# Experts of a mixture layer in steps of 1024, 1024, 1024 and 512 feed-forward columns instead of seven steps of 512

## The chip, the cores and the metric

One core of one Trainium2 chip runs the whole program. The metric is the device time of one execution in microseconds (us). A matmul on TensorE (PE) has a weight load (PEld) and a multiplication; DVE is VectorE, ACT is ScalarE, SP is SyncE, whose queue issues the weight transfers. All data is float32, and the trace shows every float32 matmul of the code as two weight loads and two matmuls.

## The reference, cut to what matters

The program computes two transformer blocks over 256 tokens of width 1024. The part that the change touches is the mixture of experts at the end of the first block: eight experts, two chosen for each token, each a gated feed-forward layer with 3584 hidden columns.

```python
def expert_block(args):
    tok, e = args
    xb = xf[tok]
    hb = jax.nn.silu(xb @ w_gate[e]) * (xb @ w_up[e])     # 1024 -> 3584
    return hb @ w_down[e]                                 # 3584 -> 1024
...
out = jnp.zeros((T, D), jnp.float32).at[row_tok].add(y)   # y: rows times the gate of the token
```

## The kernel before

**Weights.** All large weights of the program go through one ring in SBUF, `weight_ring`, of 6 slots (SLOTS) with 2048 floats on each of 128 partitions (SLOTW), so 1 MB a slot. SP fills them in a fixed order (`load`, line 304). Before it issues the load with number q it waits until `slots_used` says that PE has finished with load q - 6. PE waits for a slot's own semaphore (`landed`), does the slot's matmuls, and adds one to `slots_used`. So SP runs at most six slots ahead, and the order of the loads is the order in which PE uses them.

**One expert.** The tokens of an expert, at most 96 (CAP), lie feature-major in `hcur` (8 chunks of 128 features by 96 tokens). DVE copies them there and signals `tokens_ready`. The 3584 hidden columns are done in STEPS_M = 7 steps of 512. A step s has six slots: two of gate weights (each 4 of the 8 feature chunks by 512 columns, so rows of 512 floats in HBM), two of up weights, and two of down weights (256 rows of 1024 floats each). An expert has 42 slots.

**Engines in a step.** `gate_up_wide` (matmuls on line 723) sums gate and up into PSUM banks 2(s%2) and 2(s%2)+1, so two sets of banks take turns. ACT takes tanh of the gate bank (`step`, line 1166, into THS). DVE multiplies (1 + tanh) by gate (line 1464, into AAS, `gate_ready`) and that by up (line 1461, into HBS, `hidden_ready`). `down_wide` (matmuls on line 738) of step s-1 comes after gate and up of step s and adds into banks 4 and 5. The factor one half of silu is applied elsewhere.

**Order on PE for an expert.** Gate and up of step 0; `turn` (8 transposes of the expert before, line 749); gate and up of step 1; `scatter(0)` (line 760, adds half of the tokens of the expert before); down 0; `scatter(1)`; then a hardware loop `pe.Fori` of two passes, each with steps 2+2i and 3+2i and the downs behind them; then gate and up of step 6, down 5 and down 6. All this is the body of an outer hardware loop over the 8 experts. SP, ACT and DVE have loops of the same form.

Of the kernel before, what the change touches and what calls it, by code (L numbers as in the profile page):

```python
# [15 lines left out]
P = 128  # L16
# [7 lines left out]
SLOTS = 6  # L24
# [7 lines left out]
MCOLS = 512  # L32
STEPS_M = 3584 // MCOLS
MOE_SLOTS = 6 * STEPS_M

# [54 lines left out]
def fused_two_blocks(nc, ins, out):  # L90
# [4 lines left out]
    with ExitStack() as ctx:  # L95
# [66 lines left out]
        HBS = SC[:, 1, :, :].rearrange("p a b -> p (a b)")[:, 0:8 * CAP].rearrange("p (a f c) -> p a f c", a=2, f=4)  # L162
# [133 lines left out]
        def _(sp):  # L296
# [22 lines left out]
            def experts(wg, wu, wd):  # L319

                q0 = SLOT["moe"]

                def columns_of(w, e, s, j):
                    return w[bass.ds(e * KT + 4 * j, 4), :, bass.ds(s * MCOLS, MCOLS)].rearrange("k p n -> p k n")

                def rows_of(e, s, j):
                    return wd[bass.ds((e * (2 * STEPS_M) + s * 2 + j) * COLS, COLS), :].rearrange("(f p) n -> p f n", p=P)

                with sp.Fori(0, NEXP) as e:
                    ec = e * MOE_SLOTS  # L330
                    for j in range(2):
                        load(q0 + j, columns_of(wg, e, 0, j), 4, ec)
                    for j in range(2):
                        load(q0 + 2 + j, columns_of(wu, e, 0, j), 4, ec)
                    with sp.Fori(0, STEPS_M - 1) as i:
                        x = ec + i * 6
                        for j in range(2):
                            load(q0 + 4 + j, columns_of(wg, e, i + 1, j), 4, x)
                        for j in range(2):
                            load(q0 + 6 + j, columns_of(wu, e, i + 1, j), 4, x)  # L340
                        for j in range(2):
                            load(q0 + 8 + j, rows_of(e, i, j), 2, x)
                    for j in range(2):
                        load(q0 + MOE_SLOTS - 2 + j, rows_of(e, STEPS_M - 1, j), 2, ec)
# [203 lines left out]
        def _(pe):  # L548
# [155 lines left out]
            def moe():  # L704
# [7 lines left out]
                def gate_up_wide(q, s, rounds, wait):  # L712

                    for b in range(2):
                        bank = ps[:, 2 * (s % 2) + b, :]
                        for j in range(2):
                            w = landed(q + 2 * b + j, rounds).rearrange("p (k n) -> p k n", k=4)
                            if b == 0 and j == 0:
                                pe.wait_ge(sem("hidden_ready"), wait)
                            for m in range(4):  # L720
                                for k in range(4):
                                    for c in (0, 64):
                                        mm = pe.matmul(bank[c:c + 64, m * CAP:(m + 1) * CAP],  # L723
                                                       w[:, k, m * P + c:m * P + c + 64], hcur[:, 4 * j + k, :],
                                                       start=(j == 0 and m == 0 and k == 0), stop=(j == 1 and k == 3),
                                                       skip_group_check=True)
                            mm.then_inc(sem("slots_used"), 1)

                def down_wide(q, s, rounds, ready, start, stop):

                    for j in range(2):
                        w = landed(q + j, rounds).rearrange("p (f n) -> p f n", f=2)
                        if j == 0:
                            pe.wait_ge(sem("hidden_ready"), ready)
                        for f in range(2):
                            for d in range(KT):
                                for c in (0, 64):
                                    mm = pe.matmul(ps[c:c + 64, 4 + d // 4, (d % 4) * CAP:(d % 4 + 1) * CAP],  # L738
                                                   w[:, f, d * P + c:d * P + c + 64], HBS[:, s % 2, 2 * j + f, :],
                                                   start=(start and j == 0 and f == 0 and d % 4 == 0),  # L740
                                                   stop=(stop and j == 1 and f == 1), skip_group_check=True)
# [22 lines left out]
                with pe.Fori(0, NEXP) as e:  # L764
                    es, ea = e * (MOE_SLOTS // SLOTS), e * STEPS_M
                    pe.wait_ge(sem("tokens_ready"), e + 1)
                    gate_up_wide(q0, 0, es, a0 + ea)
                    turn(e)
                    gate_up_wide(q0 + 4, 1, es, a0 + ea)
                    scatter(0, e)  # L770
                    down_wide(q0 + 8, 0, es, a0 + 1 + ea, True, False)
                    scatter(1, e)
                    with pe.Fori(0, (STEPS_M - 2) // 2) as i:
                        for j in range(2):
                            s = 2 + j
                            x = ea + i * 2
                            gate_up_wide(q0 + 6 * s - 2, s, es + i * 2, a0 + s - 1 + x)
                            down_wide(q0 + 6 * s + 2, s - 1, es + i * 2, a0 + s + x, False, False)
                    s = STEPS_M - 1
                    gate_up_wide(q0 + 6 * s - 2, s, es, a0 + s - 1 + ea)  # L780
                    down_wide(q0 + 6 * s + 2, s - 1, es, a0 + s + ea, False, False)
                    down_wide(q0 + 6 * s + 4, s, es, a0 + s + 1 + ea, False, True)
# [339 lines left out]
        def _(act):  # L1122
# [38 lines left out]
            def step(s, q, ready, n=512, over="", buf=TH):  # L1161
# [4 lines left out]
                act.activation(buf[:, s % 2, :], ps[:, 2 * (s % 2), 0:n], ACT.Tanh, scale=0.5).then_inc(  # L1166
# [14 lines left out]
            def moe():  # L1181
                q0, a0 = SLOT["moe"], steps_done[0]
                n = 4 * CAP
# [5 lines left out]

                act.memzero(yfeat).then_inc(sem("expert_out_copied"), 1)  # L1190
                with act.Fori(0, NEXP) as e:
                    es, ea = e * MOE_SLOTS, e * STEPS_M
                    step(0, q0 + 1 + es, a0 + ea, n, buf=THS)
                    rows(e)
                    step(1, q0 + 5 + es, a0 + ea, n, buf=THS)
                    with act.Fori(0, (STEPS_M - 2) // 2) as i:
                        for j in range(2):
                            s = 2 + j
                            step(s, q0 + 6 * s - 1 + es + i * 12, a0 + s - 1 + ea + i * 2, n, buf=THS)
                    s = STEPS_M - 1  # L1200
                    step(s, q0 + 6 * s - 1 + es, a0 + s - 1 + ea, n, buf=THS)
# [231 lines left out]
        def _(dve):  # L1433
# [59 lines left out]
            def step(s, q, done, n=512, over="", th=TH, aa=AA, hb=None, up=1):  # L1493
# [3 lines left out]
                stt(aa[:, p, :], th[:, p, :], 1.0, ps[:, 2 * p, 0:n], ALU.add, ALU.mult).then_inc(  # L1497
                    sem("gate_ready" + over), 1)
                dve.wait_ge(sem("gate_ready" + over), done + 1)
                dve.wait_ge(sem("slots_used" + over), q + 1 + up)  # L1500
                h = (HB if hb is None else hb)[:, p, :, :].rearrange("p f t -> p (f t)")
                tt(h, aa[:, p, :], ps[:, 2 * p + 1, 0:n], ALU.mult).then_inc(sem("hidden_ready" + over), 1)
# [26 lines left out]
            def moe():  # L1529
                q0, a0 = SLOT["moe"], steps_done[0]  # L1530
                n = 4 * CAP
# [524 lines left out]
```

## Time and the profile before

| | before |
|---|---|
| median of 3 runs | 2909.37 us |
| lowest, highest | 2905.66, 2914.35 us |
| the profiled execution: its time | 2908.74 us |
| its span | 2907.0 us |
| experts, first to last gate/up/down matmul | 604.4 to 1602.5 us |

The span is that of the profiled execution; its own time is 1.74 us longer. Of the span the experts hold about 998 us. "Issue" is idle time of an engine for which the profile shows no releaser. The group "q8 instruction" of the DMA view is the traffic that brings program code, and "us to landing" is the median from the issue of a load to its last byte.

### The profile page before, as it was taken

The numbers are of one execution on the slowest core, as the hardware profiler recorded it, in microseconds if no ns is written. First come the engines' busy times: TensorE is split into PE (matmuls) and PEld (weight loads), VectorE is DVE, ScalarE is ACT, GpSimd is POOL, SyncE is SP. The second block draws the span as 40 slices with busy tenths as digits, with TensorE's granted clock in tenths as the row PEclk, the third lists the DMA queues.
The fourth block names the chain that finished last, engine by engine and source line by source line (L and its number), as shares of the span: only waits on it lengthen the run. The fifth ranks groups of instructions, "written<-read, shape, count | busy, mean of one in ns | idle before, by whom it ended". The sixth has DMA issues, their size and how long they took to land.

```text
span 2907.0 us, 64519 instructions
## 1 busy us (share of the span) xinstructions
PE 2653.3 (91%) x29724; PEld 2267.7 (78%) x29724; DVE 505.9 (17%) x949; ACT 284.9 (10%) x668; POOL 49.6 (2%) x117
## 2 busy tenths in 40 slices
PE   8799998799999999999999897789999997789998
PEld 7577767589989898898989776677776776677775
DVE  2210006420001000010100223222000224221001
ACT  1200003100000000000000122220000122210000
POOL 5000000000000000000000000000000000000000
PEclk9899999799999999999999898899999998899999
DMA  7234453259899999999989452123444452123442
GB/s 211 87 130 152 151 170 105 87 217 387 323 351 364 333 382 329 364 351 348 366 328 384 147 160 91 59 82 123 157 149 154 139 159 73 62 89 129 158 145 79
DMA packets 347811, 586.96 MB, mean 202 GB/s; under 512 B 13508, under 2 KB 187784, under 8 KB 347608
## 3 DMA queue, kind: packets, MB, share of 16 engines
q1 hardware_dynamic: 341400, 581.00, 57.0%
q8 instruction: 186, 3.05, 0.4%
q10 hardware_dynamic: 5728, 2.27, 0.3%
q0 software_dynamic: 480, 0.50, 0.2%
q14 instruction: 17, 0.14, 0.0%
HBM read 582.69 MB, written 1.05 MB: 201 GB/s over the span
## 4 chain that ended last, share of the span: by engine, by line
PE 89%; DVE 4%; ACT 4%; issue 3%; POOL 0%; DMA 0%; DVEq 0%; SPq 0%; ACTq 0%
PE ps L723 21%; PE ps L657 17%; PE ps L606 12%; PE ps L596 12%; PE ps L738 10%; PE ps L673 9%; PE ps L580 2%; PE ps L588 2%; PE ps L760 1%; ACT scores L1232 1%; PE ps L830 1%; PE ps L953 1%; DVE scores L1464 1%; DVE small L1601 1%; ACT heads_feat L1139 0%
## 5 line engine op out<-in xcount | busy, mean ns | idle before, releaser
L723 PE MATMUL ps<-heads_feat,weight_ring 128*64 128x96 f32 x14336 | 617.5, 249 | 37.6 <-issue 36.8
L723 PEld LDWEIGHTS ps<-heads_feat,weight_ring 128*64 128x64 f32 x14336 | 609.5, 140 | 46.7 <-issue 46.7
L657 PE MATMUL ps<-h_feat,weight_ring 128*128 128x256 f32 x2304 | 503.8, 380 | 0.0
L657 PEld LDWEIGHTS ps<-h_feat,weight_ring 128*128 128x128 f32 x2304 | 438.6, 191 | 72.5 <-issue 14.4
L606 PE MATMUL ps<-h_feat,weight_ring 128*128 128x256 f32 x1216 | 298.0, 409 | 46.2 <-ACT probs_feat L1139 45.3
L606 PEld LDWEIGHTS ps<-h_feat,weight_ring 128*128 128x128 f32 x1216 | 250.0, 208 | 88.7 <-issue 48.8
L738 PE MATMUL ps<-scores,weight_ring 128*64 128x96 f32 x7168 | 308.7, 246 | 11.1 <-issue 11.1
L738 PEld LDWEIGHTS ps<-scores,weight_ring 128*64 128x64 f32 x7168 | 300.3, 137 | 19.6 <-issue 19.6
L596 PE MATMUL ps<-weight_ring,h_feat 128*128 128x256 f32 x1312 | 292.0, 385 | 3.7 <-DVE h_feat L1461 3.1
L596 PEld LDWEIGHTS ps<-weight_ring,h_feat 128*128 128x128 f32 x1312 | 253.1, 194 | 40.1 <-DVE h_feat L1461 4.0
L673 PE MATMUL ps<-weight_ring,scores 128*128 128x512 f32 x576 | 252.6, 592 | 0.0
L1464 DVE SCALAR_TENSOR_TENSOR gelu_tmp<-gelu_tmp,ps 128x384 f32<-128x384 f32 (+1 forms) x92 | 55.8, 606 | 1067.7 <-ACT gelu_tmp L1166 1067.7
L673 PEld LDWEIGHTS ps<-weight_ring,scores 128*128 128x128 f32 x576 | 109.4, 190 | 123.7 <-issue 122.0
L1166 ACT ACTIVATE gelu_tmp<-ps 128x384 f32<-128x384 f32 (+1 forms) x92 | 48.9, 532 | 1450.3 <-PE ps L723 774.8
L1461 DVE TENSOR_TENSOR scores<-gelu_tmp,ps 128x384 f32<-128x384 f32 (+1 forms) x92 | 55.8, 606 | 429.8 <-PE ps L723 230.2
L580 PE MATMUL ps<-ident,stage 128*128 128x128 f32 x276 | 53.8, 362 | 49.1 <-ACT stage L1156 42.0
L580 PEld LDWEIGHTS ps<-ident,stage 128*128 128x128 f32 x276 | 41.5, 184 | 63.6 <-ACT stage L1156 33.0
L606 PE MATMUL ps<-heads_feat,weight_ring 128*128 128x256 f32 x384 | 83.4, 380 | 1.4 <-ACT heads_feat L1139 1.4
L606 PEld LDWEIGHTS ps<-heads_feat,weight_ring 128*128 128x128 f32 x384 | 72.8, 190 | 12.0 <-ACT heads_feat L1139 2.2
L596 PE MATMUL ps<-weight_ring,heads_feat 128*128 128x256 f32 x256 | 60.9, 400 | 8.3 <-DVE heads_feat L1461 7.6
L596 PEld LDWEIGHTS ps<-weight_ring,heads_feat 128*128 128x128 f32 x256 | 50.8, 201 | 18.3 <-DVE heads_feat L1461 5.6
L491 POOL TENSOR_TENSOR small<-small 128x2 f32<-128x2 f32 (+2 forms) x14 | 16.4, 1174 | 2757.9 <-DVE small L1475 1878.1
(265 smaller groups left out, 1066.9 us busy)
## 6 DMA issues: line engine op xcount, KB each, us to landing
weight_ring<-in_moe_w_gate SPq DMA_DIRECT2D x112, 1024.0 KB, 7.4
weight_ring<-in_moe_w_up SPq DMA_DIRECT2D x112, 1024.0 KB, 7.9
weight_ring<-in_moe_w_down SPq DMA_DIRECT2D x112, 1024.0 KB, 7.9
weight_ring<-in_w_ffn SPq DMA_DIRECT2D x66, 1024.0 KB, 5.2
weight_ring<-in_w_in SPq DMA_DIRECT2D x30, 1024.0 KB, 5.3
weight_ring<-in_w_merge SPq DMA_DIRECT2D x24, 1024.0 KB, 5.1
weight_ring<-in_ffn_w_gate SPq DMA_DIRECT2D x14, 1024.0 KB, 5.0
weight_ring<-in_ffn_w_up SPq DMA_DIRECT2D x14, 1024.0 KB, 5.0
```

The source lines that it names most:

```text
L580: mm = pe.transpose(bank[0:width, m * T + t * P:m * T + t * P + kin], src(m, t), ident[0:kin, 0:kin])
L588: mm = pe.matmul(out_[c:c + 64], lhs[:, c:c + 64], rhs, start=start, stop=stop)
L596: mm = (paired if n < P else pe.matmul)(bank[:, t * n:(t + 1) * n], lhs(k, t), w[:, k, :], start=(k == 0), stop=(k == kt - 1))
L606: mm = pe.matmul(bank[:, m * T:(m + 1) * T], w[:, k, m0 + m * P:m0 + (m + 1) * P], rhs(k), start=(k == 0), stop=(k == kt - 1))
L657: mm = pe.matmul(bank[:, m * n:(m + 1) * n], w[:, k, m * P:(m + 1) * P], rhs[:, k, :], start=(k == 0), stop=(k == KT - 1))
L673: mm = pe.matmul(ps[:, 4 + 2 * t + h, :], HB[:, s % 2, f, t * P:(t + 1) * P], w[:, f, h * 512:(h + 1) * 512], start=(start and f == 0), st ...
L723: mm = pe.matmul(bank[c:c + 64, m * CAP:(m + 1) * CAP], w[:, k, m * P + c:m * P + c + 64], hcur[:, 4 * j + k, :], start=(j == 0 and m == 0 ...
L738: mm = pe.matmul(ps[c:c + 64, 4 + d // 4, (d % 4) * CAP:(d % 4 + 1) * CAP], w[:, f, d * P + c:d * P + c + 64], HBS[:, s % 2, 2 * j + f, :] ...
L760: mm = pe.matmul(ps[:, 6 + h, :], gcur[0:CAP, t * P:(t + 1) * P], ycur[0:CAP, h * 512:(h + 1) * 512], start=True, stop=True)
L1166: act.activation(buf[:, s % 2, :], ps[:, 2 * (s % 2), 0:n], ACT.Tanh, scale=0.5).then_inc(sem("tanh_ready" + over), 1)
L1461: return dve.tensor_tensor(o, a, b, op)
L1464: return dve.scalar_tensor_tensor(out=o, in0=a, scalar=s, in1=b, op0=op0, op1=op1)
```

## The change

The same 42 slots are cut otherwise. A step of 1024 columns has four slots of gate (each 2 feature chunks by 1024 columns, so rows of 4 KB), four of up and four of down; the last step has 512 columns and is as before (two slots each, rows of 2 KB). Gate sums go to banks 0 and 1, up sums to banks 2 and 3, in every step, with no second set. tanh and the two products are each one instruction over n banks of 384 columns. DVE now does the scatter additions after step 0, not after step 1, and waits for `hidden_ready` of the step before ahead of AAS. PE's order is gate 0, turn, up 0, scatter(0), gate 1, scatter(1), up 1, outer 0, gate 2, up 2, outer 1, gate 3, up 3, outer 2, outer 3. Gate waits for `gate_ready` of the step before, up for its `hidden_ready`. The inner hardware loops are gone on all engines: each engine's code for an expert is straight, inside the loop over experts.

```diff
-MCOLS = 512
-STEPS_M = 3584 // MCOLS
-MOE_SLOTS = 6 * STEPS_M
+MOE_COLS = (1024, 1024, 1024, 512)
+STEPS_M = len(MOE_COLS)
+MOE_SLOTS = 3 * 3584 // COLS
+MOE_GATE, MOE_UP, MOE_DOWN = (0, 8, 20, 32), (4, 12, 24, 34), (16, 28, 36, 40)
...
 # SP
+                    inner(0)
+                    for s in range(1, STEPS_M):
+                        inner(s)
+                        outer(s - 1)
+                    outer(STEPS_M - 1)
...
 # PE
-                def gate_up_wide(q, s, rounds, wait):
-                    for b in range(2):
-                        bank = ps[:, 2 * (s % 2) + b, :]
...
+                def inner(first, bank0, s, rounds, name, wait):
+                    nk = SLOTW // MOE_COLS[s]
+                    for j in range(KT // nk):
+                        w = landed(q0 + first + j, rounds).rearrange("p (k n) -> p k n", k=nk)
+                        if j == 0:
+                            pe.wait_ge(sem(name), wait)
+                        for m in range(MOE_COLS[s] // P):
+                            out_ = ps[:, bank0 + m // 4, (m % 4) * CAP:(m % 4 + 1) * CAP]
+                            for k in range(nk):
+                                for c in (0, 64):
+                                    mm = pe.matmul(out_[c:c + 64], w[:, k, m * P + c:m * P + c + 64],
+                                                   hcur[:, nk * j + k, :], start=(j == 0 and m % 4 == 0 and k == 0),
+                                                   stop=(j == KT // nk - 1 and k == nk - 1), skip_group_check=True)
+                        mm.then_inc(sem("slots_used"), 1)
+                def gate(s, rounds, done):
+                    inner(MOE_GATE[s], 0, s, rounds, "gate_ready", done + s)
+                def up(s, rounds, done):
+                    inner(MOE_UP[s], 2, s, rounds, "hidden_ready", done + s)
...
-                    gate_up_wide(q0, 0, es, a0 + ea)
+                    gate(0, es, done)
                     turn(e)
-                    gate_up_wide(q0 + 4, 1, es, a0 + ea)
+                    up(0, es, done)
                     scatter(0, e)
-                    down_wide(q0 + 8, 0, es, a0 + 1 + ea, True, False)
+                    gate(1, es, done)
                     scatter(1, e)
-                    with pe.Fori(0, (STEPS_M - 2) // 2) as i:
...
+                    up(1, es, done)
+                    outer(0, es, done)
+                    for s in range(2, STEPS_M):
+                        gate(s, es, done)
+                        up(s, es, done)
+                        outer(s - 1, es, done)
+                    outer(STEPS_M - 1, es, done)
...
 # ACT
+                    act.activation(THS[:, 0:n, :], ps[:, 0:n, 0:4 * CAP], ACT.Tanh, scale=0.5).then_inc(
...
 # DVE
+                        dve.wait_ge(sem("tanh_ready"), done + s + 1)
+                        dve.wait_ge(sem("hidden_ready"), done + s)
+                        stt(AAS[:, 0:n, :], THS[:, 0:n, :], 1.0, ps[:, 0:n, 0:4 * CAP], ALU.add, ALU.mult).then_inc(
+                            sem("gate_ready"), 1)
...
+                        tt(HBS[:, s % 2, 0:4 * n, :].rearrange("p (a f) c -> p a (f c)", a=n), AAS[:, 0:n, :],
+                           ps[:, 2:2 + n, 0:4 * CAP], ALU.mult).then_inc(sem("hidden_ready"), 1)
```

## Rows read from the trace of the kernel before

**Rows 1.** The page: engines, and 40 slices of the span (72.7 us each).

```profile
PE 2653.3 (91%) x29724; PEld 2267.7 (78%) x29724; DVE 505.9 (17%) x949; ACT 284.9 (10%) x668; POOL 49.6 (2%) x117
...
PE   8799998799999999999999897789999997789998
...
DMA  7234453259899999999989452123444452123442
```

**Rows 2.** Waits of PE between 604 and 1603 us: total us, times, longest.

```profile
PE ps L723 <- issue: 36.8, 7, 5.5
PE ps L738 <- issue: 11.1, 17, 0.8
```

**Rows 3.** Timeline, steps in the loop of the third expert: start, us, engine, line.

```profile
1019.60 0.49 ACT L1166 ACTIVATE gelu_tmp<-ps 128x384 f32<-128x384 f32 x1 [19.61 <-PE ps L723]
1020.12 0.55 DVE L1464 SCALAR_TENSOR_TENSOR gelu_tmp<-gelu_tmp,ps 128x384 f32<-128x384 f32 x1 [4.67 <-ACT gelu_tmp L1166]
...
1024.53 5.45 PE L738 MATMUL ps<-scores,weight_ring 128*64 128x96 f32 x128
...
1029.81 10.73 PE L723 MATMUL ps<-heads_feat,weight_ring 128*64 128x96 f32 x256
...
1045.65 10.73 PE L723 MATMUL ps<-heads_feat,weight_ring 128*64 128x96 f32 x256
```

**Rows 4.** Timeline from the second expert's last two downs into the third expert.

```profile
961.94 1.24 PE L738 MATMUL ps<-scores,weight_ring 128*64 128x96 f32 x25
...
963.74 5.50 PE L738 MATMUL ps<-scores,weight_ring 128*64 128x96 f32 x128 [0.56 <-issue]
...
970.02 4.51 PE L738 MATMUL ps<-scores,weight_ring 128*64 128x96 f32 x103 [0.78 <-issue]
...
974.57 0.81 ACT L1203 ACTIVATE heads_feat<-ps 128x768 f32<-128x768 f32 x1 [17.12 <-PE ps L738]
979.44 13.38 PEld L723 LDWEIGHTS ps<-heads_feat,weight_ring 128*64 128x64 f32 x256 [5.10 <-issue]
979.45 13.56 PE L723 MATMUL ps<-heads_feat,weight_ring 128*64 128x96 f32 x256 [4.92 <-issue]
...
1006.68 1.22 DVE L1461 TENSOR_TENSOR x_res<-x_res,ps 128x1024 f32<-128x1024 f32 x1 [1.35 <-PE ps L760]
```

**Rows 5.** Stretches: us, PE, PEld, DVE, ACT, POOL, granted clock, DMA share, GB/s.

```profile
948.00:950.00 2.00, 2.00 (x55) 2.00 (x52) 0.00 (x0) 0.00 (x0) 0.00 (x0) 1.00 1.05 387
...
954.00:956.00 2.00, 2.00 (x54) 2.00 (x51) 0.00 (x0) 0.00 (x0) 0.00 (x0) 1.00 1.04 410
...
980.00:982.00 2.00, 2.00 (x30) 2.00 (x28) 0.00 (x0) 0.00 (x0) 0.00 (x0) 0.50 0.08 31
```

**Rows 6.** DMA in the loop's first pass, 1014 to 1046: packets, MB, share.

```profile
q8 instruction: 6, 0.10, 1.2%
```

**Rows 7.** DMA in the loop's second pass, 1046 to 1077: all packets, then the data queue's.

```profile
DMA packets 5127, 12.21 MB, mean 394 GB/s; under 512 B 191, under 2 KB 191, under 8 KB 5127
...
q1 hardware_dynamic: 5127, 12.21, 104.3%
```

**Rows 8.** DMA in the straight end of the third expert, 1077 to 1100.

```profile
q8 instruction: 4, 0.07, 1.2%
```

**Rows 9.** DMA issues early in the second expert, 886 to 900: last column us to landing.

```profile
weight_ring<-in_moe_w_gate SPq DMA_DIRECT2D x2, 1024.0 KB, 5.9
weight_ring<-in_moe_w_up SPq DMA_DIRECT2D x2, 1024.0 KB, 6.9
```

**Rows 10.** DMA issues later in the second expert, 936 to 948.

```profile
weight_ring<-in_moe_w_gate SPq DMA_DIRECT2D x2, 1024.0 KB, 8.1
weight_ring<-in_moe_w_up SPq DMA_DIRECT2D x2, 1024.0 KB, 8.4
```

**Rows 11.** Timeline of SP's queue, two slots of down weights and then four.

```profile
943.67 3.01 SPq L304 DMA_DIRECT2D weight_ring<-in_moe_w_up  x2
...
949.20 8.20 SPq L304 DMA_DIRECT2D weight_ring<-in_moe_w_down  x4
```

More of the change, by code:

```diff
@@ L729, in down_wide @@
[L729 to L734 removed]
+                def inner(first, bank0, s, rounds, name, wait):
+                    nk = SLOTW // MOE_COLS[s]
+                    for j in range(KT // nk):
+                        w = landed(q0 + first + j, rounds).rearrange("p (k n) -> p k n", k=nk)
+                        if j == 0:
+                            pe.wait_ge(sem(name), wait)
[7 more added lines that the diff above has]
+                        mm.then_inc(sem("slots_used"), 1)
@@ new lines, in gate, with outer @@
+                def gate(s, rounds, done):
+                    inner(MOE_GATE[s], 0, s, rounds, "gate_ready", done + s)
+                def up(s, rounds, done):
+                    inner(MOE_UP[s], 2, s, rounds, "hidden_ready", done + s)
+                def outer(s, rounds, done):
+                    for j in range(MOE_COLS[s] // COLS):
+                        w = landed(q0 + MOE_DOWN[s] + j, rounds).rearrange("p (f n) -> p f n", f=2)
+                        if j == 0:
+                            pe.wait_ge(sem("hidden_ready"), done + s + 1)
@@ L1159, in _, with step @@
             steps_done = [0]
-            def step(s, q, ready, n=512, over="", buf=TH):
+            def step(s, q, ready, n=512, over=""):
                 act.wait_ge(sem("slots_used" + over), q + 1)
@@ L1188, in rows, with tanh @@
                                    ACT.Copy).then_inc(sem("expert_rows_copied"), 1)
+                def tanh(s, es, done):
+                    n = MOE_COLS[s] // 512
+                    act.wait_ge(sem("slots_used"), q0 + MOE_UP[s] + es)
+                    act.wait_ge(sem("gate_ready"), done + s)
+                    act.activation(THS[:, 0:n, :], ps[:, 0:n, 0:4 * CAP], ACT.Tanh, scale=0.5).then_inc(
+                        sem("tanh_ready"), 1)
                 act.memzero(yfeat).then_inc(sem("expert_out_copied"), 1)
                 with act.Fori(0, NEXP) as e:
-                    es, ea = e * MOE_SLOTS, e * STEPS_M
-                    step(0, q0 + 1 + es, a0 + ea, n, buf=THS)
+                    es, done = e * MOE_SLOTS, a0 + e * STEPS_M
+                    tanh(0, es, done)
                     rows(e)
[L1195 to L1201, printed above, removed]
+                    for s in range(1, STEPS_M):
+                        tanh(s, es, done)
                     act.wait_ge(sem("slots_used"), q0 + MOE_SLOTS + es)
```

87 lines of the change are left out of this document (29 added, 58 removed).

## The prediction

> **What bounds the kernel now.** I read the page first. PE is busy for 91% of the span, and from about 604 to 1603 us, the experts, it stands at nine tenths or more in most slices while the DMA engines do too [rows 1]. So either of two streams could be the limit there: the matmuls or the weights. The waits of PE decide it. In those 998 us PE is idle before expert matmuls for 36.8 us in 7 pieces and for 11.1 us in 17 pieces, all "issue" [rows 2]. The 7 pieces are the 7 jumps from one expert back to the start of the outer loop's body. The 17 lie before line 738 and are the subject below.
>
> Inside a step PE has no hole. A step begins at 1029.81 and the next at 1045.65: 15.84 us for 256 matmuls of gate and up and 128 of down, so 5.28 us for two slots and 2.64 us for one [rows 3]. The data stream needs 1.049 MB in 2.64 us, 397 GB/s. In a stretch in which 2 KB rows move the DMA engines give 387, in one in which only down weights with their 4 KB rows move 410 [rows 5, 11]. So before, the weights are delivered about as fast as they are used, a little slower, and the ring's lead pays for the rest: loads land 5.9 to 6.9 us after issue early in an expert and 8.1 to 8.4 us later [rows 9, 10]. A slot is needed five slots (13.2 us) after its load can be issued, so PE never waits for data, and it could not gain directly from faster data.
>
> What it does wait for is program code. In the inner loop's first pass 6 packets of code come in, 16 KB each; one packet is thus 12 slots' 1536 instructions over 6, 256 instructions, or 128 matmuls with their loads [rows 6]. In the second pass none comes: all packets are the data queue's [rows 7]. In the straight end four come [rows 8], and there PE has its holes: 25 matmuls, a hole of 0.56, then 128 matmuls, a hole of 0.78, then 103 [rows 4]. The 128 between the holes take 963.74 to 970.02, 6.28 us, where 5.28 would do: a packet of code arrives 1.0 us too late. In the first pass, also straight and also under load, there is no hole. I read this as code packets queueing behind the weight loads, and getting later as those fall behind.
>
> **The change part by part.**
>
> *Matmuls.* 42 slots of 64 trace matmuls stay, with turn and both scatters: 0 us.
>
> *Banks and waits.* For a step of 1024 columns tanh covers 768 columns. The nearest rows are 0.81 us for an ACT copy of 768 and 0.49 for tanh of 384 [rows 3, 4], so 0.8 to 1.0. A DVE product costs 0.55 at 384 and 1.22 at 1024 [rows 3, 4], so about 0.95. From the end of a gate to `gate_ready` is then some 2.2 us, from the end of an up to `hidden_ready` some 1.3. Gate s+1 is behind up s (4 slots, 10.6 us, 5.3 in the last step); up s+1 is behind gate s+1 (10.6, and 5.3 in the last step); outer s behind up s+1. Least cover is 5.3 against 2.2. The moved scatter additions (2 x 1.22 us on DVE) end long before up 1 does, and the tanh behind `rows` has turn and up 0 as cover. So 0 us. Were there no cover, an expert would pay 4 x 3.5 = 14 us, 112 in all.
>
> *Loads.* SP issues the same 42 loads; none is moved past a wait of another kind. 28 slots of gate and up had 2 KB rows, now 24 of them have 4 KB rows. If these run as down does, the stream delivers 410 against a need of 397 instead of 387 to 410 against 397. Directly this is worth 0, since PE does not wait for data. If 4 KB rows that lie 14 KB apart ran no better than 2 KB ones, it is also 0. Its worth lies in the next item.
>
> The Trainium skill ("DMA: Bandwidth & Descriptors", section "Where 436 GB/s comes from") puts HBM to SBUF transfers at about 358 GB/s per core by the HBM side; by that rule longer rows could not speed the stream, and the third case below would be the rule. The trace's 387 and 410 do not agree with it.
>
> *Code.* The inner loop goes. Its second pass needed no code; now an expert's 42 slots need all their 21 packets from HBM, 6 more than before, each a chance to be 1.0 us late. Lower bound: none is late. Then the holes at the end of the expert go too. They cost 12.59 us from 961.94 to 974.53 against 10.73 for the like 256 matmuls: 1.86 us, times 8 is 14.9 us off (the 11.1 of the waits are the same holes by modelled ends). Upper bound: all but the first three are late from the start, 18 x 1.0, less about 2 that the first late ones cost nothing (four packets made only 1.86 us), less the 1.86 of now: +14 us an expert, +113 in all. Between these I go by the landing times: lateness came when loads landed after about 8 us and not at 6 to 7. With a stream 3% faster than PE the backlog does not build up and most packets stay in time. But 3% is thin, and every packet of code takes a DMA engine from the data for a while. I take 0.4 us an expert as what stays: 1.5 x 8 = 12 us off.
>
> The Trainium skill ("Runtime: NRT & Kernel Launch", section "Instruction fetch mechanics") says that code comes in blocks of 256 instructions, that PE holds 2048 of them, that crossing a block is mostly hidden and that a taken branch out of the held part stalls. That fits 6, 0 and 4 packets and the 7 long holes; "mostly hidden" does not fit the 0.56 and 0.78. By the rule alone nothing would be late after the change, 14.9 us off.
>
> *The jump between experts.* It stays: 36.8 / 7 = 5.26 us each. It is one code packet's way under load. If packets come 1.0 us sooner, so does this one; I take half, 0.5 x 7 = 3 us off; bounds 0 and 7.
>
> *Clock.* After the jump PE runs at half clock (granted 0.50) at 980 to 982 [rows 5], so that the first 256 matmuls take 13.56 instead of 10.73: 2.8 us [rows 3, 4]. A hole of 4.5 us should be followed by the same, so 0. If it were not, 7 x 2.8 = 20 us more come off.
>
> Sum: 0 - 12 - 3 = -15 us on 2908.7 of the profiled run, 2894; the median of the runs is 0.6 us above that run, so 2894 too.
>
> **The rivals.**
>
> *Same.* The backlog still builds, more slowly, and the same few packets at the end of each expert are late. For it: code packets themselves take room, and 387 to 410 is from short stretches. Terms: 0 to -5. Time 2904 to 2912.
>
> *Slower: code late in the second half of each expert.* Before, the second pass of the loop gave 31.7 us without code, just where landing times had risen to 8 us. If the backlog builds as before, packets are late from about slot 20 on: 22 slots, 11 packets, 11 - 2 = 9 us an expert against 1.86, +7 x 8 = +57 us, 2966. Against it: a late packet slows PE to 6.28 us for two slots, 334 GB/s, so that the stream catches up and the next packets are in time. With that, half of it or less: 2920 to 2940. It decides against the change as soon as more than four packets of an expert are late.
>
> *Faster by the clock too.* The hole at the jump shrinks below what halves the clock: 2894 - 20 = 2874. For it nothing but the size of the hole.
>
> *The single set of banks makes PE wait.* Against it are covers of 5.3 us and more; even 1 us in each of 32 steps is 32 us, 2940.
>
> **How the numbers follow.** Most code in time: 0.42. Same: 0.27. Slower by code: 0.22. Clock as well: 0.06. Banks: 0.03. A measurement of this kernel can tell 0.3%, 8.7 us, from no change. The first case is over that line in nearly all of its own range, 2886 to 2900, and the clock case too: faster 0.46. The same case and a little of both neighbours: 0.28. Slower 0.26. The range goes down to 2878, which leaves out most of the clock case, and up to 2945, which leaves out the slow case without catching up.
>
> **What would show it.** Right: q8 packets spread evenly over the expert, about 21; no "issue" holes before expert matmuls but the 7 jumps, these near 4.8 us; landing times near 5 to 7 us to the end of an expert; up to 410 GB/s in stretches of gate loads. Wrong: matmuls in groups of 128 with holes of 0.8 to 1.0 us between them, from the middle of each expert on; landing at 8 us still; or PE released by DVE at gate or up. ACT and DVE groups of 128x768 near 0.8 and 0.95 us, 24 each.

## The result, and the profile after

| | before | after |
|---|---|---|
| median of 4 runs each, side by side | 2910.46 us | 2931.03 us |
| lowest, highest | 2905.66, 2914.35 | 2927.31, 2933.43 |
| the profiled execution: its time, its span | 2908.74, 2907.0 | 2927.31, 2925.5 |
| experts, first to last gate/up/down matmul | 604.4 to 1602.5 | 608.4 to 1621.3 |

The ratio is 1.007, with a 95% interval of 1.0058 to 1.0082: the change makes the kernel 0.7% slower. The forecast was 2894 us, faster. The time lies in the stated range (2878 to 2945), but on the other side of the kernel before, in the part that the rival "slower, with catching up" had put there (2920 to 2940).

From the page of the kernel after, parts 1 to 3 and 6. Behind "q8 instruction" stand packets, MB and share; in the last rows the numbers are KB and median us from issue to landing.

```profile
PE 2661.8 (91%) x29724; PEld 2270.2 (78%) x29724; DVE 498.0 (17%) x901; ACT 281.0 (10%) x644; POOL 49.7 (2%) x117
...
PE   8799998799989999898999897789999997789998
...
q8 instruction: 234, 3.83, 0.5%
...
weight_ring<-in_moe_w_gate SPq DMA_DIRECT2D x112, 1024.0 KB, 6.4
weight_ring<-in_moe_w_up SPq DMA_DIRECT2D x112, 1024.0 KB, 6.6
weight_ring<-in_moe_w_down SPq DMA_DIRECT2D x112, 1024.0 KB, 6.5
```

PE has exactly as many matmuls and weight loads as before [rows 1], and in the slices of the experts it now shows eights where it had nines. Code packets went from 186 to 234, which is 6 more for each of 8 experts, as worked out. The loads land sooner than before, where the same three medians were 7.4, 7.9 and 7.9 us, and PE still waits longer. These medians don't show that the longer rows helped: run 1 below keeps the 2 KB rows, has still more holes, and its medians are 6.6, 6.9 and 6.5. As I read it, the queue of loads drains where PE stands more often. The waits of PE from 600 to 1640 us (total us, times, longest):

```profile
PE ps L729 <- issue: 40.1, 18, 5.6
PE ps L749 <- issue: 17.0, 26, 1.3
...
PE ps L771 <- DVE x_res L1470: 1.3, 1, 1.3
```

Against 36.8 in 7 pieces and 11.1 in 17 [rows 2] there are now 40.1 in 18 and 17.0 in 26. Seven of the 18 are the jumps; 11 are new, before gate and up matmuls, where there was none. The wait for DVE is at the very end, once in the kernel: the single set of banks never makes PE wait inside the experts. The timeline of PE, the end of the first expert and the whole second one, which begins at 734.47:

```profile
713.21 5.50 PE L749 MATMUL ps<-scores,weight_ring 128*64 128x96 f32 x128 [1.16 <-issue]
719.14 5.49 PE L749 MATMUL ps<-scores,weight_ring 128*64 128x96 f32 x127 [0.43 <-issue]
725.39 4.51 PE L749 MATMUL ps<-scores,weight_ring 128*64 128x96 f32 x103 [0.76 <-issue]
734.47 12.36 PE L729 MATMUL ps<-heads_feat,weight_ring 128*64 128x96 f32 x256 [4.57 <-issue]
...
794.18 17.24 PE L729 MATMUL ps<-heads_feat,weight_ring 128*64 128x96 f32 x413
811.77 4.26 PE L729 MATMUL ps<-heads_feat,weight_ring 128*64 128x96 f32 x98 [0.34 <-issue]
...
817.79 5.50 PE L749 MATMUL ps<-scores,weight_ring 128*64 128x96 f32 x128 [0.53 <-issue]
824.63 4.35 PE L749 MATMUL ps<-scores,weight_ring 128*64 128x96 f32 x100 [1.33 <-issue]
...
835.81 4.42 PE L729 MATMUL ps<-heads_feat,weight_ring 128*64 128x96 f32 x101 [0.41 <-issue]
839.99 6.61 PE L749 MATMUL ps<-scores,weight_ring 128*64 128x96 f32 x154
847.85 5.49 PE L749 MATMUL ps<-scores,weight_ring 128*64 128x96 f32 x127 [1.25 <-issue]
853.83 4.51 PE L749 MATMUL ps<-scores,weight_ring 128*64 128x96 f32 x103 [0.49 <-issue]
863.79 6.44 PE L729 MATMUL ps<-heads_feat,weight_ring 128*64 128x96 f32 x108 [5.45 <-issue]
```

For 77 us, to 811, the expert runs without a hole. From there on holes come one or two times 128 matmuls apart (x128 from 817.79; 100 and 155 from 824.63 to 835.81): 0.34, 0.53, 1.33, 0.41, 1.25, 0.49. They fall on the borders of the blocks of 256 instructions, the signature that [rows 4] showed with two holes and 1.34 us; here it is six and 4.35 us. Before, the first part of this stretch was the second pass of the inner loop, where no code had to come [rows 7]. The other experts are alike: of seven, the first hole comes 73 to 86 us after the expert's start, and one (the fourth) has none.

The trace has a record of each code packet, and these settle what the holes wait for. The six holes end at 811.77, 817.79, 824.63, 835.81, 847.85 and 853.83; code packets end at 810.37, 816.50, 823.33, 834.32, 846.53 and 852.56 (two more, at 828.24 and 839.82, came in time). All 37 holes of after that are not jumps end 1.2 to 1.5 us behind the end of a code packet, and the jumps 1.7 to 1.9 us behind one; the 17 of before and the 53 of run 1 do so within 1.2 to 1.6 us. A packet itself moves in about 1.0 us with holes and without (median 0.98 us in the experts of after and of run 6), so it isn't the move itself that takes longer.

The queue of loads has filled up just there. First the last column (median us to landing) of loads issued from 738 to 776 and from 790 to 802; then the stretch 790 to 802, with us, busy times, the granted clock, the DMA share and GB/s:

```profile
weight_ring<-in_moe_w_up SPq DMA_DIRECT2D x6, 1024.0 KB, 6.1
...
weight_ring<-in_moe_w_up SPq DMA_DIRECT2D x4, 1024.0 KB, 7.9
...
790.00:802.00 12.00, 12.00 (x296) 12.00 (x294) 0.00 (x0) 0.00 (x0) 0.00 (x0) 1.00 0.99 365
```

In those 12 us the only weights on their way are gate and up in rows of 4 KB, the DMA engines are busy throughout, and they deliver 365 GB/s where PE uses 397. It is so in the other experts too. Among loads that took over 6.5 us to land, so with a full queue, gate and up landed 2.93 us apart on average in after, against 2.87 before and a need of 2.64. The typical one is quick (median 2.64, before 2.71), but 26 of 112 took over 3.2 us.

Summed over the trace from each matmul's start to the next (so that the modelled ends do no harm), the jumps cost 38.5 us before and 35.9 after. All other holes in the experts cost 15.3 before and 31.6 after, 3.95 an expert. In all the experts take 998.1 and 1012.9 us: 14.8 more. The two profiled spans differ by 18.5. What is left, 3.7 us, arises ahead of the experts, whose first matmul comes 4.0 us later, in code that the change doesn't touch. Windows there show where; first the kernel before:

```profile
100.00:200.00 100.00, 92.46 (x464) 76.50 (x464) 12.70 (x21) 8.01 (x13) 0.73 (x1) 0.98 0.36 118
400.00:500.00 100.00, 92.16 (x373) 69.81 (x372) 45.42 (x99) 20.60 (x41) 0.70 (x1) 0.97 0.43 136
```

Then the kernel after:

```profile
100.00:200.00 100.00, 92.46 (x462) 76.98 (x461) 12.80 (x21) 8.01 (x13) 0.73 (x1) 0.95 0.35 116
400.00:500.00 100.00, 92.57 (x368) 70.21 (x367) 43.04 (x99) 18.85 (x37) 0.70 (x1) 0.95 0.43 137
```

The granted clock is 0.95 and 0.95 where it was 0.98 and 0.97. The ten profiles of this study have their first expert matmul between 604.4 and 609.5 us, and runs 3 and 4, which are alike there, have it at 604.5 and 609.5. So I count these 4 us as a difference of single executions and don't put them down to the change.

### The profile page after: what moved, and what is told of

Read it like the earlier page. It is cut to its first block, busy times and chain, and to the rows that moved or that the text cites. A ratio compares the mean times of both kernels' runs of the same rounds, so it can differ in the third digit from the quotient of the medians.

```text
span 2925.5 us, 64119 instructions
## 1 busy us (share of the span) xinstructions
PE 2661.8 (91%) x29724; PEld 2270.2 (78%) x29724; DVE 498.0 (17%) x901; ACT 281.0 (10%) x644; POOL 49.7 (2%) x117
## 4 chain that ended last, share of the span: by engine, by line
PE 88%; DVE 4%; issue 4%; ACT 3%; POOL 0%; DMA 0%; DVEq 0%; SPq 0%; ACTq 0%
PE ps L729 21%; PE ps L663 17%; PE ps L612 12%; PE ps L602 12%; PE ps L749 10%; PE ps L679 8%; PE ps L586 2%; PE ps L594 2%; PE ps L771 1%; ACT scores L1241 1%; PE ps L838 1%; PE ps L961 1%; DVE scores L1473 1%; DVE small L1614 1%; ACT heads_feat L1147 0%
## 5 line engine op out<-in xcount | busy, mean ns | idle before, releaser
L729 PE MATMUL ps<-heads_feat,weight_ring 128*64 128x96 f32 x14336 | 619.1, 249 | 41.0 <-issue 40.1
L729 PEld LDWEIGHTS ps<-heads_feat,weight_ring 128*64 128x64 f32 x14336 | 608.4, 139 | 59.1 <-issue 58.9
L663 PEld LDWEIGHTS ps<-h_feat,weight_ring 128*128 128x128 f32 x2304 | 438.6, 191 | 72.4 <-issue 14.3
L1473 DVE SCALAR_TENSOR_TENSOR gelu_tmp<-gelu_tmp,ps 128x512 f32<-128x512 f32 (+1 forms) x68 | 52.0, 765 | 1022.1 <-ACT gelu_tmp L1201 566.3
L1470 DVE TENSOR_TENSOR scores<-gelu_tmp,ps 128x512 f32<-128x512 f32 (+1 forms) x68 | 52.1, 766 | 454.5 <-PE ps L729 255.5
L1201 ACT ACTIVATE gelu_tmp<-ps 128x768 f32<-128x768 f32 (+1 forms) x32 | 23.4, 732 | 794.3 <-PE ps L729 794.3
L1174 ACT ACTIVATE gelu_tmp<-ps 128x512 f32<-128x512 f32 x36 | 21.5, 597 | 675.7 <-PE ps L663 675.7
```

The lines of the kernel that those rows point to most:

```text
L663: mm = pe.matmul(bank[:, m * n:(m + 1) * n], w[:, k, m * P:(m + 1) * P], rhs[:, k, :], start=(k == 0), stop=(k == KT - 1))
L729: mm = pe.matmul(out_[c:c + 64], w[:, k, m * P + c:m * P + c + 64], hcur[:, nk * j + k, :], start=(j == 0 and m % 4 == 0 and k == 0), stop ...
L1470: return dve.tensor_tensor(o, a, b, op)
L1473: return dve.scalar_tensor_tensor(out=o, in0=a, scalar=s, in1=b, op0=op0, op1=op1)
```

## The experiments

Besides the theory now held (code packets come late under a full weight queue, and straight code needs more of them) there were these rivals: the loss is in the new order and waits of the single banks; or it is in the 4 KB rows.

**1. Only the loop removed.** The kernel before, with PE's inner hardware loop written out; SP, ACT and DVE keep theirs.

```diff
-                    with pe.Fori(0, (STEPS_M - 2) // 2) as i:
+                    for i in range((STEPS_M - 2) // 2):
```

> The kernel before (seven steps of 512, rows of 2 KB, two sets of banks) with PE's inner loop of two passes written out, so that its code needs 6 more packets per expert; nothing else. Code theory (packets of program code queue behind the weight loads and come late once those have fallen behind): holes of 0.5 to 1.5 us between groups of 128 matmuls in the second half of each expert, as many as after the change or more, since 2 KB rows are slower than PE: 2925 to 2955 us. Row theory (the 4 KB rows are what makes code late): few holes beyond the two of before, 2908 to 2915. Bank or step theory (the single set of banks or the wide steps cost the time): 2908 to 2915.

Measured: 2942.77 us, ratio 1.0111 (1.0096 to 1.0126). This one line, which changes no matmul, no load and no wait, costs more than the whole change. Its waits of PE:

```profile
PE ps L723 <- issue: 52.6, 36, 5.5
PE ps L738 <- issue: 16.1, 24, 1.1
```

There are 60 pieces where before had 24, all "issue", and q8 has 234 packets as after. The interval lies wholly above that of the change (1.0058 to 1.0082): everything else in the change together gives back some 0.4%.

**2. The change with rows of 2 KB.** The steps, banks, order and straight code of after; gate and up slots are filled with 4 chunks by 512 columns.

```diff
-                            for j in range(KT // nk):
-                                load(q0 + first + j, columns_of(w, e, s, j), nk, ec)
+                            for j in range(KT * MOE_COLS[s] // SLOTW):
+                                load(q0 + first + j, columns_of(w, e, s, j), 4, ec)
```

> The changed kernel with gate and up slots of 4 feature chunks by 512 columns, so rows of 2 KB; steps, banks, order and straight code as changed. Code theory: at least as slow as the changed kernel, since the weights fall behind more: 2930 to 2960 us, landing times of 8 us. Row theory: faster than the changed kernel, 2908 to 2918. Bank or step theory: the same as the changed kernel, 2931.

Measured: 2935.44 us, 1.0088 (1.0066 to 1.0109). The intervals of this and of after overlap, so by times alone the rows' part is not settled. The landing medians are 6.7, 7.3 and 7.1 us, not the 8 that I expected, against 6.4, 6.6 and 6.5. In the two profiles the holes other than jumps are some 40 us against 31.6 and the experts 1023.0 us against 1012.9. That is the direction forecast for longer rows, but the executions of this kernel alone lie between 2922.51 and 2943.92 us, so 10 us between two single executions don't show it. Run 2 rules out only that the 4 KB rows are what costs.

**3. The change with PE's loop put back.** To make two passes equal, PE's order becomes gate s, down s-1, up s, with one buffer for the hidden values of steps 0 to 2; the additions of the scatters stand behind up 0.

```diff
-                    up(1, es, done)
-                    outer(0, es, done)
-                    for s in range(2, STEPS_M):
-                        gate(s, es, done)
-                        up(s, es, done)
-                        outer(s - 1, es, done)
-                    outer(STEPS_M - 1, es, done)
+                    with pe.Fori(0, 2) as i:
+                        gate(1, es + i * 2, done + i)
+                        outer(0, es + i * 2, done + i)
+                        up(1, es + i * 2, done + i)
+                    gate(3, es, done)
+                    up(3, es, done)
+                    outer(2, es, done)
+                    outer(3, es, done)
```

> The changed kernel with an inner loop on PE of two passes of gate s, down s-1, up s for s = 1 and 2 (12 slots of code, used twice), rows of 4 KB, single set of banks; the scatters lie in and behind up 0; two tiny matmuls per expert clear the down banks. Code theory: no code packet in the second pass, holes only in the last ten slots of an expert if at all, fewer than before since 4 KB rows keep up: 2893 to 2906 us. Row theory: 2910 or more. Bank or step theory: 2925 or more, with PE released by DVE or ACT at a gate or an up.

Measured: 2932.40 us, 1.0082 (1.0069 to 1.0096), a miss. Its waits:

```profile
PE ps L734 <- issue: 34.4, 7, 5.8
PE ps L779 <- DVE x_res L1479: 18.8, 9, 2.2
PE ps L754 <- issue: 10.3, 15, 1.3
```

The holes before gate and up are gone (7 pieces, the jumps). But my placing of the additions made a new wait: the second scatter matmul waits for DVE, whose first addition was queued behind a product that waits for up 0. That is up to 2.2 us at each of 8 turns, and run 4 gets 18.4 us back by mending it.

**4. The same, addition first.** DVE does the first scatter addition ahead of that product, and tanh is released by the end of its own gate.

```diff
-                    wide(0)
-                    added(0, e).then_inc(sem("scatter_added"), 1)
+                    wide(0, lambda: added(0, e).then_inc(sem("scatter_added"), 1))
```

> The third experiment with DVE's first scatter addition ahead of the product that waits for up 0, and tanh released by its gate: PE's 19 us of waits for DVE should go, with up to 5 us of half clock behind them. Code theory in its first form (4 KB rows keep code packets in time): 2905 us or less. Code theory in the form that the runs so far suggest (code is late in any straight stretch under load, 4 KB rows or not): the two late packets at the end of each expert stay, 2908 to 2914. Bank theory: over 2915 with PE released by DVE or ACT inside the loop.

Measured: 2913.98 us, 1.0004 (0.9991 to 1.0017): the time of the kernel before, with 1024-column steps, 4 KB rows and single banks. So the banks and their waits, the first rival, cost nothing that this measurement can tell (the interval reaches to 0.2%), and the loss of the change, 0.7%, goes when PE's loop comes back. (This kernel also differs from after in the order of up and down.) It shows too that 4 KB rows alone don't keep a straight tail in time. The timeline at the end of its second expert has the holes of [rows 4]:

```profile
839.04 5.50 PE L754 MATMUL ps<-scores,weight_ring 128*64 128x96 f32 x128 [0.47 <-issue]
845.25 5.49 PE L754 MATMUL ps<-scores,weight_ring 128*64 128x96 f32 x127 [0.71 <-issue]
850.99 4.67 PE L754 MATMUL ps<-scores,weight_ring 128*64 128x96 f32 x107 [0.25 <-issue]
```

**5. Straight code without a full weight queue.** The kernel after, all 21 code packets an expert, but each gate and up load of the 1024-column steps brings one of its two feature chunks, and each of the 512-column step one of four. The rest of the slot keeps old weights. The kernel cuts the up loads as well as the gate loads, more than the text of its expectation says; 64% of the bytes are left. `few` is `load` with `src[:, 0:1]`.

```diff
-                                load(q0 + first + j, columns_of(w, e, s, j), nk, ec)
+                                few(q0 + first + j, columns_of(w, e, s, j), nk, ec)
```

> The changed kernel with its gate loads cut: a load moves only the first of the slot's two feature chunks (the only chunk's worth for 512 columns is one of four), so the expert layer computes with stale weights; all matmuls, waits and issues stay. Code theory: the queue is light, so no hole between groups of 128 matmuls, and the holes at the jumps shrink from about 5 to 3 to 4 us: 31 us of holes and 7 to 14 of jumps less, 2886 to 2893 us. Row theory: some holes stay, 2905 to 2920. Bank or step theory: 2925 or more.

Measured: 2887.04 us, 0.9922 (0.9903 to 0.9941). Its waits of PE:

```profile
PE ps L734 <- issue: 27.0, 7, 4.6
```

And the code packets on its page:

```profile
q8 instruction: 234, 3.83, 0.6%
```

The same 234 packets, and not one hole but the jumps, and these shrink from 5.1 to 4.1 us each. It is not straight code that costs, and not its packets as such, but packets that share the DMA engines with a full weight queue.

**6. How full is too full.** The kernel after with gate and up loads that bring 7/8 of each row, the last eighth keeping old weights: 92% of the bytes. `part` is `load` with `src[:, :, 0:n]`.

```diff
-                                load(q0 + first + j, columns_of(w, e, s, j), nk, ec)
+                                part(q0 + first + j, columns_of(w, e, s, j), nk, ec, MOE_COLS[s] * 7 // 8)
```

> The changed kernel with gate and up loads that move seven eighths of each row (3.5 KB for 4 KB, 1.75 for 2), so the expert layer computes with stale last columns; 28 of 42 slots carry 7/8 of 1 MB, 92% of the bytes, a need of about 364 GB/s while PE runs without holes. It asks how thin the margin was. If code packets are late only while the weight queue is full (need close to what it can move), the holes go almost wholly, at most 8 us left of the 32: 2900 to 2908 us. If a code packet takes over 5.3 us beside any steady stream, holes stay at 25 us or more: 2924 to 2932.

Measured: 2890.80 us, 0.9939 (0.9918 to 0.996), more than I had expected of so small a cut. Its waits of PE:

```profile
PE ps L734 <- issue: 30.8, 7, 5.0
```

Code packets and a landing time from its page:

```profile
q8 instruction: 234, 3.83, 0.5%
...
weight_ring<-in_moe_w_gate SPq DMA_DIRECT2D x112, 896.0 KB, 5.7
```

The timeline of PE in its second expert:

```profile
790.58 21.29 PE L734 MATMUL ps<-heads_feat,weight_ring 128*64 128x96 f32 x512
811.70 10.73 PE L754 MATMUL ps<-scores,weight_ring 128*64 128x96 f32 x256
822.26 10.73 PE L734 MATMUL ps<-heads_feat,weight_ring 128*64 128x96 f32 x256
832.82 16.01 PE L754 MATMUL ps<-scores,weight_ring 128*64 128x96 f32 x384
853.52 6.69 PE L734 MATMUL ps<-heads_feat,weight_ring 128*64 128x96 f32 x102 [4.69 <-issue]
```

At 92% of the bytes all holes but the jumps are gone, and the landing medians are 5.7 us for gate and up and 6.1 for down. The experts take 976.9 us, 36.0 less than after, and its 31.6 us of holes and 3.4 us off its jumps are 35.0 of these. So lateness is not in proportion to the traffic: it is there when PE asks for 397 GB/s (1.049 MB in 2.64 us) and gone at 0.92 of that, 364, which is what gate and up loads got from 790 to 802 in after. Where between the two it begins was not measured.

**7. Half the instructions.** The kernel after with expert matmuls over all 128 columns of the weights instead of two of 64.

```diff
-                                for c in (0, 64):
-                                    mm = pe.matmul(out_[c:c + 64], w[:, k, m * P + c:m * P + c + 64],
-                                                   hcur[:, nk * j + k, :], ...
+                                mm = pe.matmul(out_, w[:, k, m * P:(m + 1) * P],
+                                               hcur[:, nk * j + k, :], ...
```

> The changed kernel with each pair of 64-column matmuls of the experts made one of 128 columns: half the instructions, so 11 packets of code per expert, nothing else. Code theory: no hole between expert matmuls but the jumps, which stay near 5 us. The time of a slot is open, bounded by rows: 2.64 us if one wide matmul takes what two narrow ones do (then about 2895 us), up to 3.5 us and more if the wide weight load decides (then 3180 or more). Bank or step theory: some holes of another releaser stay.

Measured: 3187.69 us, 1.0945 (1.0925 to 1.0964). The waits of PE:

```profile
PE ps L728 <- issue: 25.7, 7, 3.9
```

A stretch of its timeline:

```profile
712.57 14.46 PE L747 MATMUL ps<-scores,weight_ring 128*128 128x96 f32 x128
726.87 14.46 PE L728 MATMUL ps<-heads_feat,weight_ring 128*128 128x96 f32 x128
```

The holes are gone here too, and the jumps fall to 3.9 us, where I had expected about 5: a block of code, 128 of these matmuls, lasts 14.3 us, and the weights land 5.1 us after issue. But one trace matmul of 128 columns takes (726.87 - 712.57) / 128 = 112 ns where two of 64 take 82.5 (10.56 us from 811.70 to 822.26 in run 6 for 256). For 10752 matmuls that is some 315 us more, so this run says nothing on how the holes weigh against fewer instructions, only that they go.

**8. An expert whose code fits.** If code that comes from HBM is the cost, code that need not come should win. The kernel before, with single banks, steps of 512, rows of 2 KB, and PE's order changed so that one step (gate s, down s-1, up s) is the body of an inner loop of six passes. PE's code for an expert is then 12 slots, where before had 30 and after has 42.

```diff
+                    with pe.Fori(0, STEPS_M - 1) as i:
+                        inner(q0 + 4, 0, es + i, "gate_ready", done + 1 + i)
+                        outer(q0 + 6, es + i, done + 1 + i)
+                        inner(q0 + 8, 2, es + i, "hidden_ready", done + 1 + i)
+                    outer(q0 + MOE_SLOTS - 2, es, done + STEPS_M, True)
```

> One set of banks as in the change, steps of 512 with 2 KB rows as before, and PE's inner loop is one step (gate s, down s-1, up s) run six times, so that an expert's whole body is 12 slots of code, some 1650 instructions. Code theory: if the body stays on the chip, no code packet comes between the first expert and the last, and both kinds of holes go: 15 us of holes, 37 us of jumps and up to 20 us of half clock off 2910, some 10 us of an uncovered product before the last down and 4 us of small matmuls on: 2840 to 2865. If it doesn't stay: 7 packets per expert, jumps as before, 2900 to 2915. Bank theory: 2925 or more. Row theory says nothing against 2840 here but would put it down to 2 KB rows, which the kernel before has too.

Measured: 2853.53 us, 0.9796 (0.9781 to 0.9811): 2.0% faster than before and, by the two ratios, 2.7% faster than after. Its waits of PE:

```profile
PE ps L736 <- DVE scores L1456: 5.3, 8, 0.7
```

From its page:

```profile
q8 instruction: 58, 0.95, 0.1%
...
weight_ring<-in_moe_w_gate SPq DMA_DIRECT2D x112, 1024.0 KB, 6.5
```

The timeline of PE at the turn from the first expert to the second:

```profile
717.05 5.50 PE L736 MATMUL ps<-scores,weight_ring 128*64 128x96 f32 x128 [0.66 <-DVE scores L1456]
722.38 5.46 PE L721 MATMUL ps<-heads_feat,weight_ring 128*64 128x96 f32 x128
727.77 1.08 PE L746 MATMUL ps<-ident,heads_feat 128*96 128x128 f32 x8
```

There is no "issue" hole in the experts at all, neither in a step nor at the jump, where the next expert's gate begins at 722.38 right behind the last down. 58 packets are left in the whole kernel and none in the middle of the experts. The weights land no sooner (6.5 us) and have rows of 2 KB: neither was what held PE. Between 720.9 and 1555.9 us the windows give the granted clock:

```profile
720.90:1555.90 835.00, 824.26 (x19017) 800.06 (x19012) 79.26 (x131) 42.17 (x71) 0.00 (x0) 1.00 1.00 373
```

The granted clock stays at full level; PE stops for 0.7 us at most here, while behind each jump of about 5 us it was at half [rows 5]. Of the experts' 998.1 us 939.2 are left. The 58.9 us off are the jumps (38.5) and the holes (15.3), less what is new (5.3 of waiting for the last product, once an expert, and 8 x 0.45 = 3.6 of clearing matmuls), which leaves 14.0. That is the clock, nearly: in the kernel before the first 256 matmuls behind the seven jumps took 15.2 us more in sum than at the pace of the first expert's (10.53 us from the first start to the last).

The last row also says what comes next: the DMA engines' share is 1.00 and PE is busy for 824.26 of 835.00 us, so both streams are now full.

## Why the prediction was wrong, by its own steps

*What bounds PE: right.* In the experts PE waited for no weight load, in any run; between before, after and runs 1, 2, 5 and 6 what moves the time is "issue", code on its way. With 92% of the bytes (run 6) and with all of them 256 matmuls take the same 10.73 us.

*Matmuls, banks and waits, 0: right.* The counts are the same. tanh of 768 columns takes 0.81 us (forecast 0.8 to 1.0), a product 0.95 (about 0.95), and nothing waits for them inside the experts. Run 4 confirms it as a whole. These are ACT and DVE in the timeline of after:

```profile
746.95 0.81 ACT L1201 ACTIVATE gelu_tmp<-ps 128x768 f32<-128x768 f32 x1 [16.20 <-PE ps L729]
758.59 0.95 DVE L1470 TENSOR_TENSOR scores<-gelu_tmp,ps 128x768 f32<-128x768 f32 x1 [9.76 <-PE ps L729]
```

*Loads, directly 0: right.* PE doesn't wait for them.

*Code, -12: wrong, and this is the step that failed.* The sentences were: "With a stream 3% faster than PE the backlog does not build up and most packets stay in time", and "I take 0.4 us an expert as what stays". Measured is 3.95 us an expert against 1.9 before, so +16.3 in place of -12. Both halves of the first sentence fail in the trace of after. The stream was not faster than PE: gate and up loads in rows of 4 KB ran at 365 GB/s from 790 to 802, against a need of 397, and with a full queue landed 2.93 us apart on average against 2.64. I had taken for them the 410 that down rows had shown for 2 us; the typical load of after only just met the need, and about a quarter were slow. And so the backlog did build up: in the expert shown the loads from 738 to 776 landed after 5.0 to 6.4 us, and in every expert with holes those that landed in the 12 us before its first hole had taken 7.1 to 8.6 us.

I had also said that a code packet takes a DMA engine from the data, and had put no price on it. In run 4, whose loop has a pass without packets, gate and up loads under a full queue landed 2.99 us apart where a code packet moved in between and 2.67 where none did, and in the kernel before the like figures are 3.00 and 2.78. In after (2.92 and 2.95) and in run 1 the two don't differ, so that packets slow the weights is a hint and not shown. It would fit run 8, which has neither packets nor "issue" holes and lands its 2 KB rows after 6.5 us, where before took 7.4.

The reading of the landing times, late from about 8 us on, held roughly for the first hole. It didn't hold for the holes behind it: in run 1 the loads from 822 to 862 landed after 5.9 to 6.4 us and holes went on. And the first pass of the loop, straight and nearly without holes (one in eight experts), did not show that packets are safe under load. It lay where the queue was shorter (landings of 5.9 and 6.9 us [rows 9]).

Nor does the loop's second pass give PE a lead that lasts. In the kernel before no code packet moved from 919.3 to 954.9; the first one for the straight end started 3.5 us after the last matmul of the loop, 3.5 to 3.8 us in all eight experts, and the next two were late each time. What the second pass did was to need no code just while the queue was full. Straight code needs six packets there.

*The jump, -3: right in size, not for its reason.* 38.5 us fell to 35.9, -2.6. But in run 1, with rows of 2 KB and nothing changed but the loop, they are 36.4. So nearly all of it came without the faster rows from which I had worked it out; the number was luck. Nor is a jump "one code packet's way": in each of the seven of before two code packets ended while PE stood.

*The clock, 0: about right.* Behind the jump PE still runs at the lower level: the first 256 matmuls of the expert at 734.47 take 12.36 us against 10.73. In sum over the seven jumps this costs 13.7 us, 15.2 before: -1.6. The 2.8 a jump of the prediction was the worst of the seven; their mean is 2.2.

With the measured terms the sum is 0 + 16.3 - 2.6 - 1.6 = +12.1, against +14.8 in the experts; the last 2.7 us I don't assign.

*The rival that came true.* "Slower: code late in the second half of each expert" had the place, the mechanism, and with catching up the time, 2920 to 2940. It had put the point of decision at more than four late packets an expert; 4.6 came late on average (37 in eight experts), 2.1 before. It had the catching up right as well: the holes are 0.3 to 1.3 us and don't grow, +16 us in all and not +57, and the landing times fall again behind the first of them (8.6 us at its highest in the expert shown, 7.2 to 7.3 from 812 to 860). I gave it 0.22. The trace had the better argument for it: two places with the same load and straight code, one early in the expert and without holes, one late and with them, and between them the only stretch that needed no code, "just where landing times had risen to 8 us", as the rival's own text says.

The Trainium skill ("Runtime: NRT & Kernel Launch", section "Instruction fetch mechanics") says that PE holds 2048 instructions and that a taken branch stalls when its target isn't in the current window of two pages, which would be 512 instructions. Run 8, whose 12 slots are 1536 instructions and a few more, agrees with the first and not with so short a window: no packet and no stall at the inner or the outer jump. The same section's "mostly hidden" for crossing a block holds in runs 5, 6 and 7 and not in after or run 1, where a late block comes 5.9 to 6.8 us after the one before (719.14 less 713.21, 824.63 less 817.79 in after) and PE uses it in 5.28.

*Still open.* That the holes end with a code packet is shown, and that they go with a lighter weight stream. Why a packet starts late in a full queue is not: the trace has no record of when it was asked for. Letting SP run fewer slots ahead, with all bytes kept, would test it and was not tried. Why one expert of the eight in after (the fourth, 123.3 us against 126 to 129 for the others that end with a jump) has no late packet at all, I don't know. What makes one load in four or so land over 3.2 us behind the last one is open too. Nor was run 8 tried with 4 KB rows.

## What to carry to other kernels

Count the instructions of the busiest engine's loop body before unrolling it. Where weights stream at about the rate that the DMA engines can give, each block of code that has to come in can come late, and a loop whose body stays on the chip (12 slots, 1.5 thousand instructions here) was worth 2.0%, while unrolling a loop of two passes cost 1.1%. When a trace shows holes in one straight stretch and none in another, compare how full the queue of loads is in each, from the landing times of that stretch. A median over the whole kernel hides it: here it fell from 7.9 to 6.6 us while the holes doubled.

## What the runs showed of the hardware that was not expected

- Code comes late all at once rather than in proportion. With 364 GB/s asked of the DMA engines no block was late, with 397 six of the 21 in the expert shown were. The 8% of bytes were worth 31.6 us of holes, more than the change lost.
- PE goes on 1.2 to 1.5 us after the code packet that it lacked has landed, and 1.7 to 1.9 us after it at a jump (37 holes and 7 jumps in after).
- PE stops for a jump out of the held code for 5.1 us under a full queue, 4.1 with 64% of the weight bytes, and 3.9 with wide matmuls (sums from start to start over the 7 jumps: 35.9, 28.8 and 27.6). A lighter queue takes no more than a quarter off.
- One trace matmul of 128 weight columns and 96 tokens costs 112 ns, two of 64 columns 82.5 ns together.
